# Which weights an MoE stage prefetches before its first expert: three pieces of experts 5 and 6, and the last norm's scale and shift

## The reference, cut to what matters

```python
def hier_moe(h, lp):
    ...
    y = jnp.zeros_like(t)
    for e in range(N_EXPERTS):
        hid = jax.nn.silu(t @ lp['exp_w_gate'][e]) * (t @ lp['exp_w_up'][e])
        y = y + comb[:, e:e + 1] * (hid @ lp['exp_w_down'][e])
    return y.reshape(b, n, d)
...
    h2 = ln_plain(x) * (1 + sc2) + sh2
    x = ln_affine(DEEPNORM_ALPHA * x + g2 * hier_moe(h2, lp), lp['ln2_g'], lp['ln2_b'])
```

## Time and profile before

| | us |
|---|---|
| median of 3 runs | 664.37 (662.54 to 666.27) |
| the profiled execution: its time | 667.03 |
| its span (what the rows below divide) | 665.3 |
| busy: PE / DVE / ACT / POOL | 619.1 (93%) / 266.9 / 107.2 / 114.5 |
| DMA: moved, mean over the span | 176.50 MB, 265 GB/s |
| PE's granted clock, mean | 0.993 of full speed |

### The profile page before, as it was taken

The page is one execution under the profiler, slowest core; times in us unless marked ns, Lnnn a source line. Parts: engine busy times, 40 slices in busy tenths (PEclk is TensorE's granted clock), DMA queues, the critical chain, the costliest instruction groups (busy, mean ns, idle before and its releaser), DMA issues.

```text
span 665.3 us, 8643 instructions
## 1 busy us (share of the span) xinstructions
PE 619.1 (93%) x3423; PEld 348.1 (52%) x3423; DVE 266.9 (40%) x600; ACT 107.2 (16%) x223; POOL 114.5 (17%) x113
## 2 busy tenths in 40 slices
PE   6998999999999999999999999999999987778894
PEld 3553345546455556565554575665565543444541
DVE  4321543135534543302325866334333333222247
ACT  2001543211022322240000012111111111111000
POOL 4000000110300000000001222434334333221101
PEclk9999999999999999999999999999999999999898
DMA  9997737345030330308995089999999999999952
GB/s 340 391 330 282 253 128 254 127 132 186 24 128 9 118 109 19 96 32 244 398 404 249 32 320 355 349 418 415 412 417 417 414 415 413 416 417 418 411 226 95
DMA packets 56120, 176.50 MB, mean 265 GB/s; under 512 B 10378, under 2 KB 12458, under 8 KB 44432
## 3 DMA queue, kind: packets, MB, share of 16 engines
q1 hardware_dynamic: 39264, 143.34, 55.5%
q10 hardware_dynamic: 11152, 24.47, 10.5%
q0 software_dynamic: 5664, 8.14, 3.5%
HBM read 174.32 MB, written 11.96 MB: 280 GB/s over the span
## 4 chain that ended last, share of the span: by engine, by line
PE 70%; DMA 15%; DVE 8%; issue 3%; ACT 2%; POOL 1%; SPq 0%; ACTq 0%; DVEq 0%; POOLq 0%
PE bank L1619 13%; PE bank L1901 12%; PE bank L1608 7%; PE bank L1793 6%; PE bank L1910 5%; DMA Y<-exp_w_up 4%; PE bank L1807 4%; DMA X<-exp_w_up 4%; DMA W<-exp_w_up 4%; PE bank L1572 3%; PE bank L1532 2%; DMA Y<-w_ada 2%; PE bank L1875 2%; POOL rstd L706 1%; PE bank L1760 1%
## 5 line engine op out<-in xcount | busy, mean ns | idle before, releaser
L1901 PE MATMUL bank<-X,Y 128*64 128x256 f32 x672 | 80.6, 389 | 12.4 <-DMA X<-exp_w_up 11.4
L1619 PE MATMUL bank<-Y,W 128*128 128x384 f32 x256 | 86.6, 492 | 0.0
L1901 PEld LDWEIGHTS bank<-X,Y 128*64 128x64 f32 x672 | 51.0, 135 | 46.8 <-DMA X<-exp_w_up 18.4
L706 POOL TENSOR_TENSOR rstd<-ss,cst 128x1 f32<-128x1 f32 (+3 forms) x21 | 22.6, 1074 | 294.4 <-DVE ss L839 294.4
L1619 PEld LDWEIGHTS bank<-Y,W 128*128 128x128 f32 x256 | 47.4, 190 | 36.0 <-issue 5.6
L1608 PE MATMUL bank<-W,Y 128*128 128x512 f32 x144 | 64.0, 598 | 0.0
L749 POOL DMA_INDIRECT Y<-h_rows,gidx x31 | 40.3, 1301 | 86.0 <-PE bank L1875 80.5
L1218 DVE COPY abias<-bank 128x128 f32<-128x128 f32 x32 | 9.3, 292 | 111.5 <-PE bank L1937 111.5
L1901 PE MATMUL bank<-W,Y 128*64 128x256 f32 (+1 forms) x320 | 37.7, 340 | 7.1 <-DMA W<-exp_w_up 3.4
L754 POOL DMA_INDIRECT pair_rows<-PTr,sidx x32 | 32.9, 1029 | 64.6 <-DVE PTr L1232 64.0
L1608 PEld LDWEIGHTS bank<-W,Y 128*128 128x128 f32 x144 | 26.7, 190 | 30.9 <-issue 30.6
(11 more groups left out here) (237 smaller groups left out, 731.5 us busy)
## 6 DMA issues: line engine op xcount, KB each, us to landing
X<-exp_w_gate SPq DMA_DIRECT2D x22, 1024.0 KB, 25.5
X<-exp_w_up SPq DMA_DIRECT2D x22, 1024.0 KB, 26.3
X<-exp_w_down SPq DMA_DIRECT2D x22, 1024.0 KB
Y<-w_ada ACTq DMA_DIRECT2D x16, 1024.0 KB, 8.3
W<-w_in SPq DMA_DIRECT2D x7, 2048.0 KB, 9.2
W<-exp_w_gate SPq DMA_DIRECT2D x10, 1024.0 KB
W<-exp_w_up SPq DMA_DIRECT2D x5, 1024.0 KB
W<-exp_w_down SPq DMA_DIRECT2D x5, 1024.0 KB
```

The source lines that it names most:

```text
L706: nc.gpsimd.tensor_tensor(rstd[:, 0:n], ss[:, 0:n], const("mhalf", 0, n), ALU.pow)\
L1619: ins = mm(bank[:, 0:TOKENS], w[:, k, c * P:(c + 1) * P], hT[:, :, k, :], start=k == 0, stop=k == KT - 1)
L1901: ins = mm(bank[hh * 64:hh * 64 + 64, a:b], x_[:, c, h * 64:h * 64 + 64], rhs(hh), start=k == 0 and a == 0, stop=k == KT - 1, skip_group_c ...
```

## The change

It does four things. Expert 5's up moves to two free stretches of `Y1` (`Y1[:, 1:3, 0, :]`), and its load to right behind expert 5's gate and a wait for the last merged column. Expert 5's down moves as one piece to `Y2`'s first 2048 columns, its load ahead of the loop. Expert 6's gate (its first use of buffer 0) goes to where the last norm's scale and shift will lie, `Y2[:, 2, :]` and `Y1[:, 0, 0, :]`, in two halves, counted on `gate_in`, and is asked for ahead of the loop too; expert 6's up goes to buffer 0 as before, so the loop's first turn asks for it alone. And ACT asks for the last norm's rows in expert 6's round, behind its silu. In `gate_up` expert 6 takes the form with separate gate and up matmuls.

```diff
-        ln2 = lambda j: Y1[:, j, 0, :]
+        ln2 = lambda j: (Y2[:, TILES - 1, :], Y1[:, 0, 0, :])[j]
...
-                 views(Wflat[:, SLOTW:SLOTW + KD], y2[:, 0:KD], y2[:, KD:KD + D], merged(TILES - 1))]
+                 ([Wflat[:, SLOTW:SLOTW + KD].rearrange("p (k n) -> p k n", k=KT),
+                   Y1[:, 1:3, 0, :].rearrange("p a (k n) -> p a k n", k=KT // 2)], [y2[:, 0:D], y2[:, D:2 * D]])]
         NBUF = len(ebuf)
+        early_gate = [ln2(j).rearrange("p (k n) -> p k n", k=KT // 2) for j in range(2)]
+
+        def gate_weights(n, k):
+            return early_gate[k // 4][:, k % 4] if n == NBUF else ebuf[n % NBUF][0][0][:, k]
+
+        def up_weights(n, k):
+            up = ebuf[n % NBUF][0][1]
+            return up[:, k // 4, k % 4] if n % NBUF == PARTED else up[:, k]
...
-        def down_target(n):
-
-            return (32 if n % NBUF == PARTED else 16) * (n // NBUF + 1)
+        def gate_up_target(n):
+
+            return 32 * (n // NBUF + 1) - (16 if n >= NBUF and n % NBUF == 0 else 0)
...
             load_part(sp, "exp_w_gate", 0, PARTED, PARTED, ew_in[PARTED])
+            sp.wait_ge(S["merged_ready"], KT)
+            load_part(sp, "exp_w_up", 1, PARTED, PARTED, ew_in[PARTED])
             for n in range(3):
                 last.wait_full(sp, "wo", n, LAST_TILE)
...
             expert0.wait_full(sp, "rows")
-            load_part(sp, "exp_w_up", 1, PARTED, PARTED, ew_in[PARTED])
+            load_down(sp, PARTED, PARTED, ed_in[PARTED])
+            gate6 = pick(T["exp_w_gate"][0].rearrange("e (p k) n -> p e k n", k=KT), NBUF)
+            for j in range(2):
+                sp.dma_start(early_gate[j], gate6[:, 4 * j:4 * j + 4, :]).then_inc(S["gate_in"], 16)
...
                 sp.wait_ge(S["gu_full"], n - NBUF + 1)
-                if n < NE - 1:
+                if n == NBUF:
+                    load_part(sp, "exp_w_up", 1, n, n % NBUF, ew_in[n % NBUF])
+                elif n < NE - 1:
                     load_gate_up(sp, n, n % NBUF, ew_in[n % NBUF])
...
-                refill_down(n - 1 if n <= SERIAL else n)
+                if n > NBUF:
+                    refill_down(n - 1 if n <= SERIAL else n)
...
-            for j in range(2):
-                act.dma_start(ln2(j), (T["ln2_g"], T["ln2_b"])[j].to_broadcast([P, D])).then_inc(S["ln2_in"], 16)
             act.wait_ge(S["exp_asked"], 1)
...
                 A_(sg, gub[n % 2][:, 0:P], ACT.Silu).then_inc(S["silu_ready"], 1)
+                if n == NBUF:
+                    for j in range(2):
+                        act.dma_start(ln2(j), (T["ln2_g"], T["ln2_b"])[j].to_broadcast([P, D])).then_inc(S["ln2_in"], 16)
...
-                    if w < len(egu):
+                    if w < len(egu) and n != NBUF:
                         parts = [(0, 2 * P, lambda hh: egu[w][:, :, k, hh::2])]
                     else:
-                        parts = [(0, P, lambda hh: wg[:, k, hh::2]),
-                                 (P, 2 * P, lambda hh: wu[:, k, hh::2])]
+                        parts = [(0, P, lambda hh: gate_weights(n, k)[:, hh::2]),
+                                 (P, 2 * P, lambda hh: up_weights(n, k)[:, hh::2])]
...
             def next_gate_up(n):
                 if n < NE - 1:
-                    pe.wait_ge(ew_in[n % NBUF], (n // NBUF + 1) * 32)
+                    pe.wait_ge(ew_in[n % NBUF], gate_up_target(n))
+                if n == NBUF:
+                    pe.wait_ge(S["gate_in"], 32)
                 pe.wait_ge(S["xTe_ready"], n + 1)
```

More of the change, by code:

```diff
@@ L355, in program @@
         early = {2: X[:, 8544:8544 + KT * HALF], 1: X[:, 0:KT * HALF], 3: adabuf}
-        merged = lambda i: Y1[:, i, 0, :]
         x1 = lambda i: Y1[:, i, 1, :]
@@ L500, in load_part @@
         def load_part(eng, name, g, e, s, landed):
-            src = T[name][0].rearrange("e (p k) n -> p e k n", k=KT)
-            eng.dma_start(ebuf[s][0][g], pick(src, e)).then_inc(landed, 16)
+            src = pick(T[name][0].rearrange("e (p k) n -> p e k n", k=KT), e)
+            if s == PARTED and g == 1:
+                src = src.rearrange("p (a k) n -> p a k n", a=2)
+            eng.dma_start(ebuf[s][0][g], src).then_inc(landed, 16)
         def load_gate_up(eng, e, s, landed):
@@ L509, in load_down @@
         def load_down(eng, e, s, landed):
[L510 to L514, removed]
+            both_halves = (y2[:, 0:2 * D] if s == PARTED else whole[s][:, 2 * KD:3 * KD]).rearrange("p (h n) -> p h n", h=2)
             src = T["exp_w_down"][0].rearrange("e (p h) n -> p e h n", h=2)
             eng.dma_start(both_halves, pick(src, e)).then_inc(landed, 16)
-        def down_target(n):
-            return (32 if n % NBUF == PARTED else 16) * (n // NBUF + 1)
+        def gate_up_target(n):
+            return 32 * (n // NBUF + 1) - (16 if n >= NBUF and n % NBUF == 0 else 0)
         def pick(src, e):
@@ L1876, in tokens, with last_gate_up @@
                 ins.then_inc(done, 1)
[L1878 to L1881, removed]
+            def last_gate_up(bank, x_, n, done):
+                for landed, count, a, b, wx in ((S["gate_in"], 48, 0, P, gate_weights),
+                                                (S["up_in"], 16, P, 2 * P, up_weights)):
+                    pe.wait_ge(landed, count)
                     for k in range(KT):
@@ L1885, in last_gate_up, with gate_up @@
                             ins = mm(bank[hh * 64:hh * 64 + 64, a:b], x_[:, c, h * 64:h * 64 + 64],
-                                     wx[:, k, hh::2], start=k == 0 and a == 0, stop=k == KT - 1,
+                                     wx(n, k)[:, hh::2], start=k == 0 and a == 0, stop=k == KT - 1,
                                      skip_group_check=True)
                 ins.then_inc(done, 1)
-            def gate_up(bank, x_, w, done):
-                wg, wu = ebuf[w][0]
+            def gate_up(bank, x_, n, done):
+                w = n % NBUF
                 for k in range(KT):
                     h, c = k // 4, k % 4
-                    if w < len(egu):
+                    if w < len(egu) and n != NBUF:
                         parts = [(0, 2 * P, lambda hh: egu[w][:, :, k, hh::2])]
                     else:
-                        parts = [(0, P, lambda hh: wg[:, k, hh::2]),
-                                 (P, 2 * P, lambda hh: wu[:, k, hh::2])]
+                        parts = [(0, P, lambda hh: gate_weights(n, k)[:, hh::2]),
+                                 (P, 2 * P, lambda hh: up_weights(n, k)[:, hh::2])]
                     for a, b, rhs in parts:
@@ L1930, in next_gate_up @@
                 work = gate_up if n < NE - 1 else last_gate_up
-                work(gub[n % 2], xTe[:, n % 2], n % NBUF, S["gu_full"])
+                work(gub[n % 2], xTe[:, n % 2], n, S["gu_full"])
             def hidden(n):
@@ L1939, in next_down @@
             def next_down(n):
-                pe.wait_ge(ed_in[n % NBUF], down_target(n))
+                pe.wait_ge(ed_in[n % NBUF], 16 * (n // NBUF + 1))
                 pe.wait_ge(S["hT_ready"], n + 1)
```

## The result

The changed kernel takes 666.7 us (median of 22 runs, 664.2 to 671.0) against 664.7 for the kernel before in the same session (22 runs). The ratio is 1.0028, 95% interval 1.0015 to 1.0042: slower by some 2 us, where 661.3 was forecast; the range was 657.6 to 666.0. The profiled execution took 669.03, with a span of 667.0 (before 667.03 and 665.3). In this kernel's profile gate and up stand in L1917, the token transposes in L1891, down in L1926, SP's loads in L513 and L523, gate 6's early load in L659.

A forecast was written before the change was run, and what follows sets the result against it. The weights' stream was taken to set the pace late in the expert phase, PE itself after expert 29. Terms -4.1 + 0.4 + 0.15 + 0.5 = -3.05 us, from the median 664.37, gave 661.3; range 657.6 to 666.0.

The forecast's parts named there:

- Expert 5's down and expert 6's gate: Loads asked for at 409.73: gate 7 starts 3.15 us earlier, less 0.4 for expert 1's later gather.
- gate 7 can't be asked for before 422.96: SP's ask for expert 7's gate waits for expert 1's gate and up matmuls, so 422.96 is its earliest time.
- The sum of the stream: Net effect on the weights' stream: 3.15 - 0.4 - 2.9 = -0.15 us, about even; bounds +0.65 and -2.95.
- the change starves the stream: Rival: all bad stream bounds together lose 2.95 us; with the stop gone, 664.1 us; chance 0.05.
- Expert 5's up: Load moved from 409.73 to behind expert 5's gate at 345.02, where its 1.05 MB (2.5 us) is free.
- The last norm's scale and shift: Rows moved from 399.53 to expert 6's round, into the full weights' stream; cost taken as 2.9 us.
- PE's instructions: Code behind expert 6 shifts 64 instructions, so expert 29's stop and low clock go: 4.1 us gained, all but 0.4.
- the leftover of 0.4: PE's remaining wait for the next program block near expert 29's start, 0 to 1 us, taken as 0.4.
- The tail: After the experts, outputs wait for the last scatter, which lies in the full stream: 0.5 us lost (0 to 1).
- The stop stays: Rival: expert 29's stop isn't removed, leaving only the stream's 0.15 us; 664.5 us; chance 0.18.
- slower at the landing: Rival: PE stands at the jump's landing for a full 7.4 us block fetch; 669.4 us; chance 0.09.
- the stream wins: Rival: gate 7 finds no hole and norm rows cost no more than before; 656.9 to 658.7 us; chance 0.16.

The follow-up runs named there:

- e2: Changed kernel plus 191 empty semaphore increments on PE in rounds 8 to 26, so the jump lands at its old place in a block; 667.47 us, ratio 1.0038.
- e4: Changed kernel plus two unused matmuls in PE's wait for expert 1's gather; 665.60 us, ratio 0.9999 to the kernel before.
- e3: Changed kernel with expert 6's gate asked for only after expert 1's gather has landed; 663.87 us, ratio 0.9981 to the kernel before.
- e5: Changed kernel with expert 6's gate behind expert 1's gather and the last norm's rows asked for in round 30; 662.53 us, ratio 0.9961.
- e8: Kernel before with only the last norm's rows asked for in expert 6's round; 667.15 us, ratio 1.0020.
- e6: Changed kernel with expert 5's down and expert 6's gate asked for in the loop's first turn as before; 667.58 us, ratio 1.0022.
- e7: Changed kernel with only expert 5's up early and the last norm's rows asked for in round 30; 666.06 us, ratio 1.0005.
- e9: Kernel before plus 150 empty semaphore increments on PE in rounds 12 to 26; 664.54 us, ratio 0.9982.
- e1: Kernel before plus 65 empty semaphore increments on PE in rounds 17 to 26, shifting later code as the change does; 664.10 us, ratio 0.9983.
- e11: e1 plus 256 more increments, 16 in each of rounds 1 to 16; 664.08 us, ratio 0.9988 to the kernel before.
- e12: e5 plus 256 increments, 16 in each of rounds 1 to 16; 662.99 us, ratio 0.9969 to the kernel before.
- e10: e5 plus 85 empty semaphore increments on PE in rounds 12 to 26; 663.28 us, ratio 0.9964 to the kernel before.

## Why the prediction was wrong

**Step "Expert 5's down and expert 6's gate", the gather late by 0 to 2, taken as 0.4: mis-sized.** It came 1.65 us late beside 2.1 MB. From issue to landing it took 5.8, 5.8 and 5.9 us (after, e2, e4), 3.0 beside 1.05 MB (e3, e5, e8), and 3.0 with no load of SP's beside it as well (e6, e7). The reason given for 0.4, that the gather had been issued into busy engines before as well, looked at the moment of issue and not at how much lay in front of its last bytes. Nor had it run beside the end of 1.05 MB alone: up to 412 the last norm's rows were still moving on ACT's queue, and code that is the same there gave 3.9 (e9), 4.8 (e1) and 5.2 us (e11). The Trainium skill (DMA: Bandwidth & Descriptors, Queues, rings and completion order) states that each DMA engine goes round between its queues by whole packets. The 3.0 us of e3, in which the gather had to share with 1.05 MB only, fit that but don't prove it.

**The same step, "gate 7 can't be asked for before 422.96": right as a bound, and where it failed.** I moved the bound by the gather's 0.4 us and by nothing else. What I didn't think of is that PE, which had hardly stood there (0.29 us), would stand 1.77 us, and that its clock would then be 0.50 through just the 32 matmuls on whose end SP waits. 1.65 us of a late gather became 4.46 us of a late ask, into a queue that the early loads had left empty. e4 shows the clock's share, 3.2 us, by keeping PE busy; e3 shows the whole. The profile before held the hint: PE at 0.57 after a stand of 2.1 us. I used it for expert 29's matmuls alone.

**The sum of the stream, -0.15 with a worst bound of -2.95:** the stream lost 3.8 us at expert 28. The rival "the change starves the stream" had the mechanism and too small a price, since its bounds held no clock. The view I had asked for ("engines partly idle between 421 and 425") came out wider, 423 to 428.5.

**Step "Expert 5's up", 2.5 us free: not true in itself.** e7 shows that up 5 alone moves nothing. In the count of bytes it was harmless, as I set the sum by when SP may ask for gate 7, and down 5 and gate 6 were worth what that count gives them: 3.15 predicted, 3.3 and 3.1 measured, once nothing delays the ask.

**Step "The last norm's scale and shift", 2.9: right as a mechanism, somewhat too dear.** It was 2.3, 2.5 and 2.8 in three pairs of kernels; the other price that I had worked out, 2.5 by the weights' rate, was the better one.

**Step "PE's instructions", -4.1 + 0.4: mechanism right, size wrong.** Place of the stop, its length and its end by moving the code are shown by e1 and e2. Why the block isn't there in time is not: the 7.4 us that I took for a fetch stand in no run. The block's packet is on a DMA engine from 616.0 to 617.0 in the kernel before, and PE goes on at 618.42. But its 4.1 us was one execution's: the stop is 2.06 to 2.25, and the low clock behind it (4.03 us for 2.44, 1.6 of the 4.1) isn't there in e2 and e8. For the leftover of 0.4, a wait at the edge of the block, the chain after shows none. In its place stand 1.6 us of another kind: with the block edge moved ahead, the 26th packet of the program falls into the weights' stream, and the weights land that much later. Net, e1 says 0.9 us (0 to 2.2 by its interval) for what I had put at 3.7. I had counted a block's packet as something that PE waits for and not as something that takes its place on a DMA engine.

**Step "The tail", 0.5: about right in size.** From the end of expert 29's gate and up to the span's end before has 42.9 us. After has 43.2, e1 and e4, which get there 3.5 and 2.2 us earlier, 43.5, e11 (3.5 earlier) 42.9. The four kernels that ask for the norm rows in round 30 have more: 44.4 (e5 and e12), 44.3 (e10) and 44.7 (e7), against 42.8 to 43.7 in the ten others. It isn't an early arrival that does it: e7 and e4 get there at the same time. So the rows cost some 1 us at the end, beside the last scatter and the reading back of the outputs, and that is why the medians give less than the stream for moving them.

**The base.** The profiled execution of before (667.03) lay 2.3 us above the median of its later runs. Part of that is likely the low clock behind the stop (1.6 us), which isn't in every execution. The forecast took off the 2.7 us between that execution and the median shown, and also the whole stop with its low clock, so that part counted twice.

Together, in medians against the kernel before, one step at a time: moving the stop away gives -0.9 (e1). With up 5 early and the norm rows at the end it is +0.3 (e7), a step of +1.2, in which the tail's 1.2 us show. Down 5 and gate 6 ahead of the loop, behind the gather, make it -3.3 (e5), a step of -3.5. The norm rows in round 6 make it -1.1 (e3), +2.1, and gate 6 asked for ahead of the gather +2.0 (after), +3.1. Each step has an interval of some 1.6 us to either side: the -3.5 and the +3.1 are clear of it, the +1.2 is not, and of the norm rows' price only e8 (0.2 to 2.4) says by itself that it isn't nothing.

**The rivals.** "The stop stays" fell with e1, "slower at the landing" with the unbroken 64 matmuls at 619.91, and "the stream wins" with the late ask; e5, which takes the late ask and the norm rows away, is where it would have been right in part: its stream is 2.7 us ahead of that of the kernel before. Of the signs that I named, the missing gap came as put, the norm rows went out at 458.8 (named 455), and expert 5's up, asked for at 345.5, landed at 363.1, 1.1 us past the 362 named, which cost nothing. The waits for up weights, 17.4 us for 16.4, didn't tell of the stream's 3.8 us, because the stream fell behind while PE itself was late.

What stays open is why the 26th packet delays the weights by 1.6 us and the 25th doesn't. That its DMA engine lies behind already would fit, but no view tells the engines apart, and the effect was not traced beyond its place. Nor was it tried to shorten the code that is jumped over, which would move the landing without a packet in the stream.

## What to carry to other kernels

Before a load is brought forward, look for the latency-bound transfer that it will run beside (here a gather of 64 rows), then at which engine waits for that one and what its clock does after standing: the load belongs behind it, which turned 2.0 us lost into 1.1 gained here. Bytes moved into an empty stretch were worth something here only where the next ask had less behind it; what counts is the moment when the list of asks is next allowed to go on. A start in one profiled execution is worth comparing only from a common point ahead of it: here executions lay up to 1.2 us apart where their code was the same (SP's first ask at 416.06 in e1, 417.25 in e9). And take a term of a sum from more than one execution when a clock level is part of it.

## What the runs showed of the hardware that I had not expected

- The same 32 matmuls that take 3.85 us took 6.49 us behind a stand of 1.77 us (after), 5.44 behind one of 0.76 (e1), 5.04 behind 1.82 (e2) and 5.44 behind 3.14 (e9), with the clock at or near 0.50 in part of them. In expert 29, 64 matmuls behind a wait of 1.8 us took 3.86 us after the change and 5.46 in e3. And behind the stop of 2.06 us the clock fell in the kernel before and stayed at the upper level in e8, as it did behind 2.25 us in e2. The length of a stand alone doesn't tell.
- A jump can land so near the end of a block of PE's program that the next one isn't there: 2.06 and 2.25 us of standing 26 matmuls behind the landing. The Trainium skill (Runtime: NRT & Kernel Launch, Instruction fetch mechanics) calls the crossing of a block mostly hidden. In straight code the chains show no stop at one; behind this jump they do.
- A block's packet takes one DMA engine 1.0 to 1.1 us, and with one particular packet out of the ones in the stream the weights landed 1.6 us later.
- A semaphore increment on PE isn't free: 16 of them made a round 0.9 us longer (7.16 for 6.26), some 56 ns each.
